# First expert's token list by TensorE and its rows gathered in the output stage: one layer step with a mixture of experts, on one core

## What is computed

```python
def hier_moe(h, W_rg, b_rg, W_re, b_re, W_gate_e, W_up_e, W_down_e):
    ...
    pg = jax.nn.softmax((xt @ W_rg + b_rg).astype(jnp.float32), axis=-1)
    g_w, g_idx = lax.top_k(pg, 1)
    ...
    pe = jax.nn.softmax(el_sel, axis=-1)
    e_w, e_loc = lax.top_k(pe, TOP_K)
    ...
    for e in range(N_EXPERTS):
        hid = jax.nn.silu(xt @ W_gate_e[e]) * (xt @ W_up_e[e])
        y = y + combine[:, e:e + 1] * (hid @ W_down_e[e])
```

## Time and profile before

| | |
|---|---|
| median of 3 runs | 1248.89 us (1248.06 to 1253.66) |
| profiled execution, its own time | 1253.62 us |
| its span, first to last instruction | 1251.8 us |
| PE busy (share of span) | 1099.6 us (88%) |
| DVE / ACT / POOL busy | 708.2 (57%) / 601.5 (48%) / 109.2 us (9%) |
| mean granted clock of PE | 0.942 of full |

### The profile page before, as it was taken

One profiled execution on the slowest core, in us unless ns is written; L12 is line 12 of the kernel. 1 busy time (PEld: TensorE's weight loads), 2 busy tenths in 40 slices (PEclk: granted clock), 3 DMA queues, 4 the chain that ended last, 5 costly groups with the idle time before them and its releaser, 6 DMA issues. The chain is left out here.

```text
span 1251.8 us, 26501 instructions
## 1 busy us (share of the span) xinstructions
PE 1099.6 (88%) x8820; PEld 902.6 (72%) x8821; DVE 708.2 (57%) x1321; ACT 601.5 (48%) x1226; POOL 109.2 (9%) x237
## 2 busy tenths in 40 slices
PE   4589998999989999899957999539999998999946
PEld 4588787977889778887846878326877776777722
DVE  3533555235632556335546675756987674877638
ACT  5533445334543444434444222146877664767533
POOL 0000000000000000000000011121011101110140
PEclk8789999999999999999988999759999999999968
DMA  8532222132220421223207342359999996999565
GB/s 334 190 91 73 79 81 61 35 112 59 86 70 17 124 85 35 65 72 112 81 23 247 112 138 73 107 194 311 358 395 360 325 332 220 359 337 328 204 238 207
DMA packets 202405, 210.63 MB, mean 168 GB/s; under 512 B 15612, under 2 KB 169076, under 8 KB 202036
## 3 DMA queue, kind: packets, MB, share of 16 engines
q1 hardware_dynamic: 183120, 177.25, 42.7%
q0 software_dynamic: 5712, 18.23, 4.0%
q10 hardware_dynamic: 13492, 13.96, 3.1%
HBM read 185.32 MB, written 24.08 MB: 167 GB/s over the span
## 5 line engine op out<-in xcount | busy, mean ns | idle before, releaser
L2023 DVE TENSOR_TENSOR experts_w_lo<-all_raw,experts_w_hi 128x2048 fp32r<-128x2048 f32 x48 | 109.5, 2283 | 4.9 <-ACT experts_w_hi L1904 4.9
L2023 DVE TENSOR_TENSOR experts_w_lo<-all_raw_more,experts_w_hi 128x2048 fp32r<-128x2048 f32 x48 | 108.3, 2285 | 7.0 <-ACT experts_w_hi L1904 7.0
L910 PE MATMUL early_ps_proj<-mixers_w_hi,early_h_hi 128*128 128x512 f32 x256 | 106.4, 416 | 2.5 <-ACT mixers_decay L743 2.5
L2191 PE MATMUL experts_ps_g<-experts_w_hi,experts_x_hi 128*128 128x512 f32 x256 | 104.8, 409 | 2.2 <-DVE experts_x_lo L2029 2.2
L912 PE MATMUL early_ps_proj<-mixers_w_hi,early_h_lo 128*128 128x512 f32 x256 | 101.2, 395 | 0.0
L2193 PE MATMUL experts_ps_g<-experts_w_hi,experts_x_lo 128*128 128x512 f32 x256 | 101.1, 395 | 0.0
L2192 PE MATMUL experts_ps_g<-experts_w_lo,experts_x_hi 128*128 128x512 f32 x256 | 100.8, 394 | 0.0
L911 PE MATMUL early_ps_proj<-mixers_w_lo,early_h_hi 128*128 128x512 f32 x256 | 100.7, 393 | 0.0
L1200 DVE TENSOR_TENSOR mixers_qd_t<-mixers_turned,early_tables 128x128 f32<-128x128 f32 (+1 forms) x36 | 10.1, 281 | 152.7 <-ACT mixers_turned L791 135.3
L1904 ACT ACTIVATE experts_w_hi<-all_raw 128x2048 fp32r<-128x2048 f32 x48 | 91.5, 1909 | 5.5 <-DMA all_raw<-in_W_up_e_dram 4.6
L1904 ACT ACTIVATE experts_w_hi<-all_raw_more 128x2048 fp32r<-128x2048 f32 x48 | 91.6, 1912 | 2.2 <-DMA all_raw_more<-in_W_up_e_dram 1.6
(11 more groups left out here) (365 smaller groups left out, 2796.9 us busy)
## 6 DMA issues: line engine op xcount, KB each, us to landing
all_raw_more<-in_W_down_e_dram SPq DMA_DIRECT2D x128, 256.0 KB, 5.8
all_raw<-in_W_gate_e_dram SPq DMA_DIRECT2D x96, 256.0 KB, 5.6
all_raw<-in_W_up_e_dram SPq DMA_DIRECT2D x96, 256.0 KB, 6.8
all_raw<-in_W_in_dram SPq DMA_DIRECT2D x32, 512.0 KB, 4.8
all_raw<-in_W_ada_dram SPq DMA_DIRECT2D x32, 512.0 KB, 5.0
condition_w_ada_in<-in_W_ada_dram SPq DMA_DIRECT2D x4, 2048.0 KB, 12.1
...
```

The costliest lines, as they stand in the source:

```text
L910: pe.matmul(out, xhi, whi, start=(k == 0), stop=False)
L2023: dve.tensor_tensor(w_lo[:, 2 * p:2 * p + 2], raw_pair[p], f32(w_hi[:, 2 * p:2 * p + 2]), ALU.subtract).then_inc(lo_done, 1)
L2191: pe.matmul(out, x_hi[:, k, :], w_hi[:, c, at], start=(k == 0), stop=False)
```

## The change

- **Token list of expert 0 on chip.** `at_place[t, i, r]` is 1 where token t of tile i has rank r in expert 0 (DVE, one compare per group against a constant row of 0 to 127), `id_first` is the token's number if it chose expert 0, else 0. PE multiplies the two, nine products added up in one column (`first_list`): tiles 0 to 6 while DVE works on the last group, tiles 7 and 8 after it. DVE casts the column to integers (`s.index`).
- **Gather in the output stage.** POOL issues the gather of expert 0's 128 rows there, ahead of the last group's four list writes; it waits for `s.index` and for all ten stores on `h_stored`. The wait for `scattered` moves from POOL's end of the output stage to SP, ahead of the load of `lists`, in the experts. POOL's first instruction of the experts is a load of the plan that waits for `lists`.
- **Ten high parts early.** ACT loads its table for the experts and makes five pairs (`READY = 5`) of expert 0's `w_hi` at the end of the output stage, after all 12 chunks have arrived. `w_hi` and `x_rows` get memory that is not used by the output stage. In the experts ACT starts with the rows.
- **Order on DVE in the experts**: one split, the rows, five splits (before: two, the rows, four).
- The count of all tokens and the new list use a projection bank of PSUM instead of `ps_l`; `slot` is made with three instructions instead of six; the constants grow by 128 columns.

```diff
 POOL, output stage
             for n, (lo, hi) in enumerate(GROUPS):
                 pool.wait_ge(slots_done, n + 2)
+                if hi == NT:
+                    pool.wait_ge(h_stored, 16 * NT + 16)
+                    pool.indirect_dma_start(out=s.x_rows[:, :], out_offset=None, in_=s.h_scr[:, :],
+                                            in_offset=bass.IndirectOffsetOnAxis(ap=s.index[:, 0:1], axis=0))\
+                        .then_inc(s.x_in, 16)
+                    pool.wait_ge(slots_done, n + 3)
...
-            pool.wait_ge(scattered, 16 * 2 * NT)
 ACT, output stage
             exponentials(len(GROUPS) - 1)
+            act.preload_act_table_set("silu_and_others")
+            act.wait_ge(mm_done, 2 * NT)
+            act.wait_ge(prefetched, 32 * CHUNKS)
+            for p in range(READY):
+                pair = raw[:, 2 * p:2 * p + 2] if 2 * p < RAW else s.more[:, 2 * p - RAW:2 * p - RAW + 2]
+                act.activation(s.w_hi[:, 2 * p:2 * p + 2], pair, ACT.Copy)
 PE, output stage
+            def list_first(lo, hi):
+                for i in range(lo, hi):
+                    last = pe.matmul(first_list, at_place[:, i, :], id_first[:, i:i + 1], start=(i == 0), stop=(i == NT - 1))
+                return last
+            begun = GROUPS[-1][0]
+            pe.wait_ge(gated, NT)
+            pe.wait_ge(slots_done, len(GROUPS))
+            list_first(0, begun)
             count(len(GROUPS) - 1)
-            pe.wait_ge(l_read, NT)
-            pe.matmul(ps_l[:, 0:NE], s.const("ones"), before[:, NT, :], start=True, stop=True)\
-              .then_inc(counted, 1)
+            pe.matmul(n_tokens, s.const("ones"), before[:, NT, :], start=True, stop=True).then_inc(counted, 1)
+            pe.wait_ge(both_done, len(GROUPS) + 1)
+            list_first(begun, NT).then_inc(counted, 1)
 DVE, choose and enter of each group
                 then(dve.tensor_tensor(both[:, T], chosen[:, 0, T], chosen[:, 1, T], ALU.add))
+                dve.tensor_tensor(id_first[:, T], both[:, T, 0], s.const("token", lo, hi), ALU.mult)
...
+                one = dve.tensor_tensor(at_place[:, T, :], s.const("places").unsqueeze(1).broadcast_to([P, N, P]),
+                                        rank_of[:, T, 0:1].broadcast_to([P, N, P]), ALU.is_equal)
+                if hi == NT:
+                    one.then_inc(both_done, 1)
+                of_chosen(rank[:, :, T], rank_of[:, T])
+                if hi == NT:
+                    dve.wait_ge(counted, len(GROUPS) + 2)
+                    dve.tensor_copy(s.index[:, :], first_list).then_inc(slots_done, 1)
 SP, experts
-            sp.dma_start(lists[:, :], s.list_scr.rearrange("(p n) o -> p (n o)", p=P)).then_inc(lists_in, 16)
             for n in range(CH // 2):
                 sp.sem_inc(raw_in[n], 64)
+            sp.wait_ge(s.scattered, 16 * 2 * NT)
+            sp.dma_start(lists[:, :], s.list_scr.rearrange("(p n) o -> p (n o)", p=P)).then_inc(lists_in, 16)
 POOL, experts
-            gather(slice(0, 1), P, 1)
             gather_rests(0, True)
 ACT, experts
-            act.preload_act_table_set("silu_and_others")
+            act.sem_inc(hi_done, READY)
...
-            for p in range(3):
-                split(0, p)
             x_high(0)
...
-            for p in range(3, PAIRS):
+            for p in range(READY, PAIRS):
                 split(0, p)
 DVE, experts
-            for p in range(2):
-                split(0, p)
+            split(0, 0)
             x_low(0)
+            split(0, 1)
             split(0, 2)
```

58 lines of the change are left out of this document (33 added, 25 removed).

## The result

The changed kernel takes **1255.99 us** (median of 20; 1251.60 to 1260.49), the kernel before beside it 1251.91 us (median of 20): ratio **1.0031**, 95% interval 1.0019 to 1.0043. It is slower by about 3.9 us where 2 us of gain were forecast, and lies above the forecast's range of 1243.0 to 1250.6. By the half per cent named in the prediction it counts as no change. The forecast's 1246.9 us was taken off a median of three executions, 1248.89; over twenty the same kernel's median is 1251.91, so 3.0 of the 9.1 us between forecast and result are the scatter of the base.

A forecast was written before the change was run, and what follows sets the result against it. PE was taken to bound the experts, with a hole ahead of them. Of 11.2 us there, 7.1 go back to ACT, leaving 4.0; less a 2.0 us stall, 1248.89 falls to 1246.9 us, range 1243 to 1250.6.

The forecast's parts named there:

- half per cent: Whole kernel: a measurement can tell about 0.5%, 6.2 us, from no change; chance of landing within it 0.85.
- the base: Time of the kernel before: median 1248.89 us, from which the shift worked out on the profiled execution (1253.62 us) was taken.
- the first rest: Experts: expert 1's first 32 rest rows, needed by PE at 842.8, land at 844.9 behind held copy and gather; stall 2.0 us.
- ACT sets the barrier: End of output stage: ACT leaves last after five high parts (9.2 us, to 830.0); experts begin at 830.4, 7.1 us later.
- Rows there, first product 4.15 us behind the barrier: Start of experts: rows have landed, PE turns them at once and reaches its first product 4.15 us later, at 834.6.
- 4.0 + 0.6: First product 4.0 us sooner overall, though the path to the last stored tile is 0.6 us longer on DVE.
- rival 2: Experts, one split later: POOL ready only after 836.6, rest rows land at 847.1, stall 4.3, change +0.3, 1249.2 us; chance 0.15.
- DVE's additions: Output stage: two more DVE instructions per group cost 0 to 0.9 us on the path to the last stored tile, taken as 0.6.
- 2 and 3: rival 2, and the same mechanism two splits on: landing 849.3, stall 6.5, change +2.5, 1251.4 us; chance 0.06 for the latter.

The follow-up runs named there:

- e8: e1 with four instead of five early pairs on ACT (READY = 4): ratio 0.9996 to the kernel before.
- e6: The kernel before, with DVE's first two weight splits waiting until POOL's queue has issued its first gather of the experts: ratio 1.0004.
- e13: The kernel before, with DVE's first two splits waiting for a memset that POOL runs after its first gather, so the gather is never held: 1250.84 us, ratio 0.9992.
- e14: The kernel before, with POOL's first gather waiting for ACT's first high part and a memset, so it is always held: 1254.47 us, ratio 1.0015.
- e1: The changed kernel, with POOL's wait for the lists moved from ahead of its plan loads to right ahead of its index copy: ratio 1.0013 to the kernel before.
- e5: e1, with DVE's five splits waiting until POOL's queue has issued the first gather of the experts: ratio 1.0021 to the kernel before.
- e9: The changed kernel plus an unused 320-byte tensor that puts the buffers back on the 512-byte grid: ratio 1.0021 to the kernel before.
- e11: The changed kernel with the edits of e8 and e9 together: ratio 0.9982 to the kernel before.
- e10: The kernel before plus an unused 192-byte tensor that shifts the buffers off the 512-byte grid: ratio 1.0015.
- e18: The kernel before, with the load of the sample's modulation rows given its own semaphore, so DVE's first norm doesn't wait for it: ratio 0.9977.

## Why the prediction was wrong, point by point

The step that failed is the price of the first rest: PE's stall was put at 2.0 us and was 6.2 (point 3), with 1.6 us of lower clock behind it that stood nowhere in the sum. Two more terms were off: what is lost ahead of the last h tile (point 4) and the base (point 5).

1. **ACT sets the barrier: right.** 9.1 us for five parts (9.2 forecast), barrier right behind, and in e8's rows one part comes off it.
2. **Rows there, first product 4.15 us behind the barrier: right** (4.13). The seam gained 6.4 us where 4.0 + 0.6 were reckoned, since the last chunks arrived 1.6 us sooner after the store than in before (825.8 - 809.5 = 16.3, against 820.2 - 802.3 = 17.9). Why they did wasn't looked into.
3. **The first rest: the mechanism right, the term mis-sized: 6.2 us for 2.0.** POOL needed 3.9 us from the landing of `lists` to its copy, not 2.5, so the copy missed one split (rival 2's condition). And from the end of the split that held the gather to the landing of the rows it took 7.7 us (845.8 to 853.5: 0.8 until the gather ended, as in the earlier trace rows, and 6.9 from there), not 6.0. Rival 2's stall of 4.3 and these 1.7 make 6.0 of the 6.2 us. The sum left out that the clock falls while PE stands: 1.6 us more.
4. **DVE's additions: 0.6 us is near what is seen directly, but it is not all.** The fourth interval between h stores is 14.5 us in three of the six profiles without tables and 14.8 to 14.9 in two of the twelve with early ones, four other intervals are longer by up to 0.1. But in the other three of six it is 15.5 to 15.6, and in the other ten of twelve 15.7 to 15.9: the step of a microsecond goes with stretches at the lower clock behind a gap of PE, and with the tables it was there more often. Those gaps did not grow: PE's waits for DVE in the projection are 3.1 to 3.5 us in all twenty profiles, 3.3 in before. In the changed kernel:

```profile
PE output_ps_o L1542 <- DVE output_o_lo L1583: 3.2, 2, 1.9
```

What grew is the time at the lower clock. Stretch by stretch of 1 us from the projection's first product to the store, PE's busy time times the share of the clock that it lacked adds up to 4.0 us in before, 8.1 in the changed kernel and 3.2 to 9.3 in all twenty; without it this part takes 135.5 to 138.8 us everywhere. So of the 6.0 us between the first two profiles 4.1 are lower clock and 1.3 the longer gap at the first tile (2.95 for 1.63); 0.6 are left, the size that was forecast for DVE. Ahead of the store the four profiles of before, e6, e13 and e14 have 141.2 us in the mean, the four of the changed kernel's own code there (after, e1, e5, e8) 144.4. So some 3 us are lost there. Why the clock fell more often, and what the tables, the shifted buffers (1.3 to 1.9 us by e9 to e11) and chance have to do with it, stays open.
5. **The base: the step that I did not see.** I reckoned the gain against a profiled execution in which the first gather was held, and took its working to the median. e13 and e14 suggest that the kernel before is more often unheld than held: about 2 of the 3.6 us are already had there without the change. The rows say so with less scatter: from the last h tile's store to the first down product it took 52.9 to 54.2 us in the four near copies with the gather unheld (e6, e10, e13, e18), 56.5 and 57.2 in the two with it held (before, e14), and 56.0 in the changed kernel. So the change gains 0.5 us there on the profiled base and loses 2 to 3 on an unheld one. It is a tie of less than 0.1 us, in rows that I quoted side by side.

The sum, with the sizes of the runs: seam -6.4, experts +5.8, ahead some +3, base some +2 gives +4.4, for 3.9 measured. Its last two terms are estimates, from scattered profiles and from ratios whose intervals overlap. Against the held kernel (e14, 1.0015) the change costs only 0.0016.

Of the rivals, 2 and 3 named the mechanism; none named the base. The range was too narrow because every case in it took the seam of one execution, and the median of three, as the kernel's.
